# A mixture-of-experts stage in a one-core kernel: weights as the left operand over 96 slots, fixed first blocks, first loads and zeros issued earlier

## The reference, cut to what matters

```python
def hier_moe(h, w_rg, b_rg, w_re, b_re, w_up, w_down):
    g_logits = (h @ w_rg + b_rg).astype(jnp.float32)
    p_g = jax.nn.softmax(g_logits, axis=-1)
    g_sel = jnp.argmax(g_logits, axis=-1)
    p_sel = jnp.take_along_axis(p_g, g_sel[:, None], axis=1)
    e_logits = (h @ w_re + b_re).astype(jnp.float32).reshape(T, N_GROUPS, EXPERTS_PER_GROUP)
    e_in = jnp.take_along_axis(e_logits, g_sel[:, None, None], axis=1)[:, 0]
    top_v, top_i = lax.top_k(e_in, TOP_K_INNER)
    w2 = jax.nn.softmax(top_v, axis=-1) * p_sel
    ...
    for n in range(N_EXPERTS):
        a, b = jnp.split(h @ w_up[n], 2, axis=-1)
        out = out + combine[:, n:n + 1] * ((jax.nn.silu(a) * b) @ w_down[n])
    return out
```

## Time and profile before

| what | value |
|---|---|
| median of 3 runs | 2861.12 us (2857.35 to 2861.81) |
| the profiled execution, its own time | 2859.85 us |
| its span, first to last instruction | 2857.7 us |
| TensorE (PE) busy, share of the span | 2512.4 us, 88% |
| weight loads (PEld) busy | 1898.8 us, 66% |
| mean granted TensorE clock | 0.938 of 2.4 GHz |
| the stage that the change touches | about 2396 us to the end |

### The profile page before, as it was taken

How to read it: one execution, slowest core, us unless ns; L and a number is a source line. 1 busy time by engine, 2 the same in 40 slices (tenths; PEclk the granted TensorE clock), 3 DMA queues, 4 the chain that set the end, 5 groups by cost and what they waited for, 6 DMA issues and landing times. The chain is left out here.

```text
span 2857.7 us, 30665 instructions
## 1 busy us (share of the span) xinstructions
PE 2512.4 (88%) x10883; PEld 1898.8 (66%) x10883; DVE 1407.8 (49%) x2108; ACT 975.4 (34%) x1672; POOL 287.8 (10%) x288
## 2 busy tenths in 40 slices
PE   5999996698999988998899897898798787699995
PEld 4777785576887776767788785687576566344442
DVE  4766435645554444634555535187895743111112
ACT  3422332334453335323545423332335431011111
POOL 0000001100000000000000000454240430011001
PEclk9999997899999998999999998999898897799998
DMA  4122231122333222203233322232020110899996
GB/s 138 67 81 89 89 103 74 60 74 74 102 89 118 103 76 71 78 30 103 74 101 90 132 74 74 90 108 89 15 104 1 52 67 32 310 366 365 372 367 247
DMA packets 215017, 339.18 MB, mean 119 GB/s; under 512 B 13910, under 2 KB 110046, under 8 KB 214910
## 3 DMA queue, kind: packets, MB, share of 16 engines
q1 hardware_dynamic: 209149, 316.79, 32.3%
q0 software_dynamic: 5760, 20.97, 2.0%
HBM read 304.18 MB, written 33.55 MB: 118 GB/s over the span
## 5 line engine op out<-in xcount | busy, mean ns | idle before, releaser
L366 PE MATMUL ps<-ffn_h_hi,ffn_w_hi 128*128 128x512 f32 x704 | 275.6, 391 | 10.5 <-DVE ffn_h_lo L361 10.5
L367 PE MATMUL ps<-ffn_h_lo,ffn_w_hi 128*128 128x512 f32 x704 | 275.3, 391 | 0.0
L368 PE MATMUL ps<-ffn_h_hi,ffn_w_lo 128*128 128x512 f32 x704 | 275.0, 391 | 0.0
L366 PE MATMUL ps<-wo_hi,lhs_hi 128*128 128x512 f32 x608 | 242.3, 398 | 34.0 <-DVE lhs_lo L361 34.0
L367 PE MATMUL ps<-wo_lo,lhs_hi 128*128 128x512 f32 x608 | 240.9, 396 | 0.0
L368 PE MATMUL ps<-wo_hi,lhs_lo 128*128 128x512 f32 x608 | 240.5, 396 | 0.0
L361 POOL TENSOR_TENSOR w_lo<-ring,w_hi 128x512 fp32r<-128x512 f32 (+1 forms) x112 | 159.5, 1425 | 762.3 <-ACT w_hi L518 761.3
L3855 PE MATMUL ps<-ring,expert_x 128*128 128x512 f32 x512 | 228.8, 600 | 8.4 <-issue 5.7
L3855 PEld LDWEIGHTS ps<-ring,expert_x 128*128 128x128 f32 x512 | 98.3, 193 | 133.2 <-issue 129.8
L361 DVE TENSOR_TENSOR wo_lo<-ring,wo_hi 128x1024 fp32r<-128x1024 f32 x76 | 93.0, 1224 | 185.4 <-ACT wo_hi L653 185.4
L2245 DVE SCALAR_TENSOR_TENSOR y_tmp<-ps,pcol,y_tmp 128x511 f32<-128x511 f32 x88 | 61.9, 745 | 219.8 <-ACT y_tmp L2217 219.8
(11 more groups left out here) (609 smaller groups left out, 5168.6 us busy)
## 6 DMA issues: line engine op xcount, KB each, us to landing
ring<-in_w_up SPq DMA_DIRECT2D x32, 2048.0 KB, 11.9
ring<-in_ffn_w_up SPq DMA_DIRECT2D x88, 512.0 KB, 4.9
moe_down<-in_w_down SPq DMA_DIRECT2D x32, 1024.0 KB, 9.9
ring<-in_ab_w_in SPq DMA_DIRECT2D x13, 2048.0 KB, 7.9
ring<-in_w_in SPq DMA_DIRECT2D x11, 2048.0 KB, 7.8
ring<-in_ffn_w_down SPq DMA_DIRECT2D x10, 2048.0 KB, 8.0
expert_results<-expert_y SPq DMA_DIRECT2D x32, 512.0 KB, 10.0
ring<-in_c_w_in SPq DMA_DIRECT2D x6, 2048.0 KB, 8.0
```

What stands on the lines that cost most here:

```text
L366: nc.tensor.matmul(out, left[0], right[0], start=start, stop=False, **more)
L367: nc.tensor.matmul(out, left[0], right[1], start=False, stop=False, **more)
L368: return nc.tensor.matmul(out, left[1], right[0], start=False, stop=stop, **more)
```

## The change

Blocks are 96 rows instead of 128. The first block of expert e is always block e, also if it is empty; slots beyond an expert's 96th go to blocks from 32 on. In `first` the up weights are the left operand in four pieces of 128 columns and the 96 token columns the right one, so that the hidden values come out already turned: `turn_hidden` and its copy go. As blocks 0 and 1 are always experts 0 and 1, their four loads are issued in `route`, behind the store of the rows; and as only blocks from 32 on can be unused, these ten are zeroed by one DMA in `place`, whether used or not.

```diff
@@ route
             sp.dma_start(rows_dram.rearrange("(t p) d -> p t d", p=P), rows).then_inc(k.param_loaded.sem, 16)
+            prefetch(sp)
             sp.wait_ge(*k.param_loaded(16))
@@ place
-NB = 2 * -(-((SLOTS + NE * (P - 1)) // P) // 2)
+ROWS = 96
+MOST = -(-T // ROWS)
+NB = 2 * -(-(NE + SLOTS // ROWS) // 2)
...
+        @block.sync
+        def _(sp):
+            sp.wait_ge(*k.sa(1))
+            sp.dma_start(y_dram[NE * ROWS:, :].rearrange("(s p) d -> p s d", p=ROWS),
+                         zeros[0:ROWS, :].rearrange("p (o d) -> p o d", o=1).to_broadcast([ROWS, NB - NE, D])).then_inc(y_zeroed, 16)
...
-            nc.vector.tensor_scalar(r.blocks[:, :], count, 0.0, None, ALU.is_gt)
-            for n in range(1, T // P):
+            nc.vector.tensor_scalar(r.blocks[:, :], count, float(ROWS), None, ALU.is_gt)
+            for n in range(2, MOST):
...
-                nc.vector.tensor_scalar(r.is_slot[:, n, :], r.iota[:, :], r.rank[:, n:n + 1], None, ALU.is_equal)
+                nc.vector.tensor_scalar(r.is_slot[:, n, :], r.iota[:, 0:ROWS], r.rank[:, n:n + 1], None, ALU.is_equal)
@@ experts, SyncE
-            for n in range(2):
-                expert = expert_of(n)
-                load_up(n, expert)
-                load_down(n, expert)
-
             before = pair_before_last(nc.sync)
-            with sp.Fori(0, NB // 2 - 1) as i:
-                with sp.If(before < i):
-                    sp.dma_start(y_dram[bass.ds(i * (2 * P) + 2 * P, 2 * P), :]...)
...
+            sp.wait_ge(e.y_zeroed, 16)
             each_block(sp, before, step)
@@ experts, TensorE
-                    last = nc.tensor.transpose(k.ps[:, XB + c // NT, (c % NT) * P:(c % NT + 1) * P], e.rows[:, s, c * P:(c + 1) * P], k.ident[:, :])
+                    last = nc.tensor.transpose(k.ps[:, XB + c // NT, (c % NT) * ROWS:(c % NT + 1) * ROWS], e.rows[0:ROWS, s, c * P:(c + 1) * P], k.ident[0:ROWS, 0:ROWS])
...
-                for c in range(KD):
-                    last = nc.tensor.matmul(k.ps[:, UB + s, :], e.x[:, s, c, :], up[s][:, c, :], start=(c == 0), stop=(c == KD - 1))
+                for m in range(2 * FTE):
+                    for c in range(KD):
+                        last = nc.tensor.matmul(k.ps[:, UB + s, m * ROWS:(m + 1) * ROWS], up[s][:, c, m * P:(m + 1) * P], e.x[:, s, c, :],
+                                                start=(c == 0), stop=(c == KD - 1), skip_group_check=True)
                 last.then_inc(e.up_done, 1)
 
-            def turn_hidden(n):
...
-                        last = nc.tensor.matmul(k.ps[:, YB + half, :], e.hid_cm[:, s, j, :], dn[s][:, j, half * BANK:(half + 1) * BANK],
+                        last = nc.tensor.matmul(k.ps[0:ROWS, YB + half, :], e.hid[:, s, j * ROWS:(j + 1) * ROWS], dn[s][:, j, half * BANK:(half + 1) * BANK],
                                                 start=(j == 0), stop=(j == FTE - 1))
...
             def step(n):
                 if inside(n, 1):
                     first(later(n, 1))
-                turn_hidden(n)
                 if inside(n, 2):
                     turn_rows(later(n, 2))
                 second(n)
@@ experts, ScalarE
-                act.wait_ge(e.hid_turned, at_block(n, 1, 1))
-                if not early(n, 2):
-                    act.wait_ge(e.down_done, at_block(n, 1, -1))
-                nc.scalar.copy(e.hid_cm[:, s, :, :], k.ps[:, HB, 0:EF].rearrange("p (j m) -> p j m", j=FTE)).then_inc(e.hid_ready, 1)
                 act.wait_ge(e.down_done, at_block(n, 1, 1))
@@ moe
+        def first_experts(sp):
+            for n in range(2):
+                sp.dma_start(up[n], A["w_up_2"][0][n].rearrange("(t p) n -> p t n", p=P)).then_inc(e.up_loaded[n], 16)
+                sp.dma_start(dn[n], A["w_down_2"][0][n].rearrange("(t p) n -> p t n", p=P)).then_inc(e.down_loaded[n], 16)
+        route(k, wr, r, k.ytmp[:, :, :], rows_dram, first_experts)
```

More of the change, by code:

```diff
@@ L3503, in mixers2, with route @@
     project_out(k, lambda n: k.h[:, n, :], KD, A["w_o_2"][0], None, next_gain, after=after, scratch=k.ytmp)
-def route(k, wr, r, rows, rows_dram):
+def route(k, wr, r, rows, rows_dram, prefetch):
     nc = k.nc
@@ L3644, in _ @@
             for n in range(2 * NT):
-                last = nc.tensor.matmul(k.ps[:, 1, 0:NB], r.is_slot[:, n, :], r.is_block[:, n, :], start=(n == 0), stop=(n == 2 * NT - 1))
+                last = nc.tensor.matmul(k.ps[0:ROWS, 1, 0:NB], r.is_slot[:, n, :], r.is_block[:, n, :], start=(n == 0), stop=(n == 2 * NT - 1))
             last.then_inc(k.pb.sem, 1)
@@ L3674, in _ @@
             dve.drain()
-            rank = [r.picked[:, 2 * s, :, 0] for s in range(2)]
-            first = [r.picked[:, 2 * s + 1, :, 0] for s in range(2)]
+            rank, beyond, own = ([r.picked[:, 3 * s + n, :, 0] for s in range(2)] for n in range(3))
             for s in range(2):
@@ L3704, in _ @@
             dve.drain()
-            nc.vector.tensor_scalar(r.pairs[:, :], r.iota[:, 0:NB // 2], 2.0, r.end[:, NE - 1:NE], ALU.mult, ALU.is_lt)
+            nc.vector.tensor_tensor(r.expert_f[:, :, 0], r.expert_f[:, :, 0], r.own[:, :], ALU.add)
+            nc.vector.tensor_scalar(r.pairs[:, :], r.iota[:, 0:NB // 2], 2.0, r.total[:, 0:1], ALU.mult, ALU.is_lt)
             dve.drain()
@@ L3717, in place @@
     k.pb.close(1)
+    k.sa.close(1)
 def at_block(n, times=1, more=0):
@@ L3912, in step @@
                 for half in range(2):
-                    last = nc.scalar.copy(e.y[:, s, half * BANK:(half + 1) * BANK], k.ps[:, YB + half, :])
+                    last = nc.scalar.copy(e.y[0:ROWS, s, half * BANK:(half + 1) * BANK], k.ps[0:ROWS, YB + half, :])
                 last.then_inc(e.y_ready, 1)
@@ L4013, in moe @@
         r.blocks, r.end, r.start = (sb("moe_" + name, [P, NE], to=c) for name in ("blocks", "block_end", "block_start"))
-        r.pick = sb("moe_pick", [P, 4, NT, NE], to=c)
-        r.picked = sb("moe_picked", [P, 4, NT, 1], to=c)
-        r.rank, r.block, r.full, r.row_f = (sb("moe_" + name, [P, 2 * NT], to=c) for name in ("rank", "block", "full", "row_f"))
+        r.pick = sb("moe_pick", [P, 6, NT, NE], to=c)
+        r.picked = sb("moe_picked", [P, 6, NT, 1], to=c)
+        r.rank, r.block, r.full, r.row_f, r.over = (sb("moe_" + name, [P, 2 * NT], to=c) for name in ("rank", "block", "full", "row_f", "over"))
+        r.beyond, r.own = (sb("moe_" + name, [P, NB], to=c) for name in ("beyond", "own"))
+        r.total = sb("moe_total", [P, 1], to=c)
         r.row = sb("moe_row", [P, 2 * NT], I32, to=c)
         r.token_id = sb("moe_token_id", [P, NT], to=c)
-        r.is_slot = sb("moe_is_slot", [P, 2 * NT, P], to=c)
+        r.is_slot = sb("moe_is_slot", [P, 2 * NT, ROWS], to=c)
         r.is_block = sb("moe_is_block", [P, 2 * NT, NB], to=c)
```

88 lines of the change are left out of this document (42 added, 46 removed).

## The result

| | before | after |
|---|---|---|
| median | 2859.23 us (4 runs, 2856.49 to 2861.81) | 2841.94 us (4 runs, 2840.42 to 2843.92) |
| ratio, 95% interval | | 0.9936 (0.9923 to 0.9948) |
| profiled execution, its span | 2857.7 us | 2841.7 us |

The account below looks back on a forecast made before the run. TensorE was taken to set the pace, DMA just keeping up. Middle -0.5, start -9.8 (`place` included) and tail -1.2 sum to -11.5, rounded to -12 us: 2847.8 profiled, 2849 as median; 8-in-10 range 2843 to 2867.

Parts of the forecast that it names:

- Up products, 64 x 0.1115 = 7.14 less 0.05: `first` per block: 64 records paced by their weight loads, 7.14 us against 6.87, 0.05 of it hidden.
- Rival 3: Up products in `first`: weight loads hide, `first` takes 5.4 us, DMA bounds, -21 us more, 2827; chance 0.03.
- The 8 of rows stay (0.87; also bound by their load of 128 columns): Eight row transposes per block in `experts`: load-bound, so still 0.87 us with 96 rows.
- The start, -9.8 us: Start of `experts`, `place` included: quicker gather and no wait before block 2's up products, -9.8 us together.
- `route` at no cost: Early loads in `route`: only the rows, first in the queue, are waited for; 0, at most +3 us.
- a load issued late behind the zeros: Block 2's `first` before the change: the explanation given for its 5.68 us wait, expected to vanish.
- Rival 1: Blocks 0 and 1: clock stays low through their up products, 13.7 us each, whole time 2862; chance 0.35.
- Rival 2: Every block's up stream: clock falls, +110 us if half runs low; or slower pitch, +7; chance 0.08.
- Rival 4: Early loads don't help: gather itself takes 8 us or prefetch holds up `route` by 3; 2856; chance 0.07.
- Share below 0.97: Middle of `experts`: DMA share expected in the changed profile, as the sign that DMA gets slack.
- The tail, -1.2: End of `experts`: last `first` to `second` 7.15 us instead of 8.14, -1.0, and a smaller last store, -0.2.
- The last store is a quarter smaller, -0.2: Tail: the last block's store moves a quarter less, saving 0.2 us.

Follow-up runs that it names:

- run 5: The changed kernel with the old order of operands (rows left, weights right, `turn_hidden` and its copy back), 96 rows kept: 2840.75 us, ratio 0.9937.
- run 14: The changed kernel with the old order of operands, plus matmuls that nobody reads on the idle TensorE (6, 12, 6): 2837.64 us, ratio 0.9922.
- run 1: The changed kernel measured once more, as yardstick for the others on its chip: 2843.36 us (5 runs), ratio 0.994.
- run 3: The changed kernel with the first four loads and the zeros both back at the head of `experts`: 2857.18 us, ratio 0.9991.
- run 4: The changed kernel with only the zeros back at the head of `experts`, the four loads still in `route`: 2849.62 us, ratio 0.996.
- run 10: The changed kernel, blocks still 96 rows, with up products over only the first 88 columns: 2855.29 us, ratio 0.9978.
- run 8: The changed kernel with up products over only 64 of a block's 96 columns: 2853.72 us, ratio 0.9979.
- run 9: The changed kernel with blocks of 88 rows instead of 96, zeros for twelve blocks instead of ten: 2862.84 us, ratio 1.0012.
- run 2: The changed kernel with only the four first loads back at the head of `experts`, zeros still in `place`: 2845.2 us, ratio 0.9948.
- run 7: The changed kernel with every second of the eight contraction pieces of the up products left out, all transfers kept: 2802.84 us, ratio 0.9803.
- run 6: The changed kernel with blocks of 128 rows instead of 96: 2849.1 us, ratio 0.9965.
- run 13: The changed kernel with blocks of 88 rows and added matmuls that nobody reads, 10 ahead of the first transposes: 2861.49 us, ratio 1.0003.

## Why the prediction was wrong by 7 us, point by point

- **Up products, 64 x 0.1115 = 7.14 less 0.05: right.** 7.12 measured, and 7.10 to 7.14 with 64, 88 and 128 columns. The exchange is worth nothing per block, and 2 us once, in the tail (runs 5, 14). Rival 3 is out: 96 columns came no faster than 64 or 128. The estimate of 83 to 85 ns from the isolated gap in the Trainium skill ("TensorE: Matmul & The Clock Gate", "Back-to-back issue gap") doesn't hold here; the trace shows 111.
- **"The 8 of rows stay (0.87; also bound by their load of 128 columns)": the step that failed.** Transposes still load 128 columns, yet eight take 0.66 us with 96 rows, 0.61 with 88 and 0.88 with 128: 82, 76 and 110 ns each. They scale with the block's rows, which are at once the rows of that load and the columns that move; no run separates the two, as the moving matrix of a transpose is square. I had carried the pitch of ordinary matmuls over to transposes because both stood near 110 ns at 128. The trace of the kernel before already had a row against it, at a clock of 1.00:

```profile
51.67 0.32 PEld L1166 LDWEIGHTS ps<-ident,q_region 64*128 64x128 f32 x4 [0.35 <-issue]
```

  These are transposes of 64 rows, also with loads of 128 columns, and the loads start some 61 ns apart (0.32 less the last one's 0.138, over three). The mis-priced term is 0.21 us a block: the middle gave 5.2 us where 0.5 was predicted. The range allowed 5 us for the pitch of the up records but nothing for this price.
- **The start, -9.8 us: right in its mechanism, 10.6 measured, with some luck.** Gather to reader 4.28 as predicted; block 0 at 2449.67 (2449.6 predicted), 9.18 long (9.6, with run 1's 10.52 on the other side of it, so that the clock's rise alone moves this term by 1.4 us); block 1 at 2460.63 (2461.4); block 2 at 2471.95 (2472.8), without a wait. `place` 1.75 us longer against 1.6, after taking off the 0.24 us by which all before it was later. `route` at no cost, also right: SyncE's fifth issue took 7.4 us, but under the router's product. What the prediction called "a load issued late behind the zeros" is confirmed by run 3; that the zeros can strike at two places, the gather or block 2's load, by what else is in the queue, it did not see (runs 3 and 4).
- **Rival 1, the low clock: did not happen, but its price was right.** It had block 1's products at 2466.5 and block 2's at 2486.2; run 10 has them at 2465.17 and 2485.03. Its 2862 is 7 above that run's 2855, mostly through the same transposes. That the wide `second` would raise the clock was right too: it rose 2.8 us into it (2483.0) in run 10 and 3.5 us in run 8. The sentence "no row says on which side" was just: with 96 columns the clock rose after 3.8 to 6.8 us, with 88 and 64 not in two blocks of 14 us. What the Trainium skill says in "The HAM clock gate", that sustained matmuls raise the clock however many they are, agrees with the change and not with runs 8, 9 and 10, in which TensorE was busy all of 13.7 us at 0.50.
- **Rival 2: out.** The clock is 1.00 from 2453.5 to the end of TensorE's work, and period and pitch never slow. But one reading against it was wrong: the 24 us of the earlier trace rows are not made of 64- and 128-column records alone. 24 of their 160 records are 384 or 512 columns wide (L2851) and stand between the narrow ones, so that row said nothing on a stream of narrow records by itself. **Rival 4: out**, by run 2.
- **DMA: the slack was there, what was to show it was wrong.** "Share below 0.97" was to show it; the share is 1.02, at fewer bytes. Run 7 puts the limit at 10.1 us per block, below the 10.7 that had been worked out from 368 GB/s.
- **The tail, -1.2: 0.2 in the end.** The 7.15 us from the last `first` to `second` came as predicted. "The last store is a quarter smaller, -0.2" had the wrong sign: from the end of the last copy to `combine`'s first gather, where the last store lies, it is 4.38 us instead of 4.01. It is 3.97 in run 6 with 128 rows, 4.35 to 4.38 in all runs with 96, and 4.53 to 4.59 with 88, so it grows as the block's rows get fewer; why was not tried. From that gather to the end it is 23.3 us instead of 22.5, but this stretch is 22.1 to 23.6 in the runs with 96 rows and 22.2 in the one with 128, so one trace of each kernel can't say that the change made it longer.
- **The sum.** Of the 7 us, 4.0 lie in the spans (16.0 measured, 12 predicted: 4.7 from the middle, 0.8 from the start, less 1.0 for the tail and 0.5 for rounding, each from one execution); 1.3 between the spans and the medians, which differ by 17.3; and 1.9 in the median of before, 2861.12 in the runs shown and 2859.23 with one more.

## What to carry to other kernels

A transfer that nobody waits for belongs where the queues are idle: here 3.9 MB of zeros in front of a gather and a weight load cost more than everything else that the change touched, and exchanging the operands of the largest product gave nothing per block. Price a transpose from transposes and a matmul from matmuls, even where one size makes them look alike. Compare stretches that begin behind the unchanged part, since the whole time carries its scatter (5 us here). And when records get narrower, look at the granted clock of a run at that very width before trusting it: leaving out eight unused columns made this kernel 12 us slower.

## What the runs showed that I had not expected

- Narrower records, lower clock: 64- and 88-column streams ran twice 13.7 us at 0.50 where the 96-column one was granted 1.00 after 3.8 to 6.8 us (runs 8, 10). Matmuls added beforehand didn't help the 88-column one: the clock fell again in the pauses before it (run 13).
- DMA of 88 rows is slow: the zeros of 4.3 MB began at 179 GB/s and a share of 0.67, against 322 at 1.00 for 96 rows and 420 at 1.02 for 128; in the middle 335 to 342 GB/s against some 350 at nearly the same share.
- A gather of 0.4 MB issued 1.1 us behind 3.9 MB of writes on another queue took 11.76 us to its reader, against 4.28 on quiet queues (run 4).
- A share of DMA of 1.02 went with 353 GB/s where TensorE set the pace and 1.04 with 389 where DMA did (run 7): only the rate under starvation told the limit.
